# Two-block transformer kernel: the running sum of the later modulation rows goes from VectorE to ScalarE and GpSimd

## The chip, the core and the metric

The kernel runs on one core of one Trainium2 chip. The metric is device time in microseconds (us) of one launch, median of a few runs. The engines are named as in the profile: PE is TensorE (PEld its weight loads), ACT is ScalarE, DVE is VectorE, POOL is GpSimd and SP is SyncE, which issues most of the DMAs. Each engine works through its own instructions in order and meets the others only through semaphores.

## What is computed

The reference runs two blocks on 256 tokens of width 2048. What matters here is the first, and in it the modulation: one row vector times a 2048 x 12288 matrix.

```python
mod = c_act @ w_ada[layer] + b_ada[layer]            # c_act = silu(c), one row of 2048
sh1, sc1, gt1, sh2, sc2, gt2 = jnp.split(mod[:, None, :], N_MOD, axis=-1)
h = rmsnorm(x, g_mix[layer]) * (1 + sc1) + sh1
x = x + (1 + gt1) * mixer(h, positions, ...)          # sb attention, dsa attention, merge, w_o
h = rmsnorm(x, g_ffn[layer]) * (1 + sc2) + sh2
x = x + (1 + gt2) * conv_ffn(h, ...)
```

`sh1` and `sc1` are needed before anything else. The other four parts, 8192 columns, are needed only after the merge, so the kernel computes them beside the attentions: this is the "late" work.

## The kernel before

Weights are f32. For each unit (128 x 2048 of a weight matrix, 1 MB, loaded by SP into one of up to four slots of `ring`) ACT rounds it in two halves of 128x1024 to `whi` (`round_unit`, L355), DVE subtracts to get the rest `wlo` (`rest_unit`, L362), and PE multiplies in three passes (`threefold`, L415 to L417). `whi` and `wlo` hold two units. A half of unit u may be rounded once PE is through the same half of unit u-2, and semaphore `used` says so. `ahead` rounds the first two units of the next iteration.

The first block's mixer has three stages in which late work runs.

- `sb`: five passes of a loop body over four pairs of heads. Pass i projects pair i (units 0 to 5) and attends pair i-1.
- `dsa`: the same for the second attention, after a stage for its index (`ki`, `qi`).
- `merge`: eight iterations of six units. In each, ACT takes two pairs of sigmoids (L1480) behind its rounding; the first pair and the second pair of banks are then combined by DVE.

The late work is 16 blocks of 512 columns. Block b has 16 lines of 128x512 (one for each 128 rows of `w_ada`), and one block falls into each iteration: blocks 0 to 3 in `sb`, 4 to 7 in `dsa`, 8 to 15 in `merge`. POOL issues the load of each line (`late_loads`, L2435) into `late_ring`, which has four slots. DVE multiplies the line by its column of `cact` and adds it to the only accumulator, `late_acc` (`late`, L1816 for line 0, L1819 for the others). A slot is loaded again when DVE has used it (`late_used`). When all 16 lines are in, PE adds up the partitions (`late_sum`, L763), at a fixed place in its order: behind units 0 and 1 of the next iteration. Until then line 0 of the next block may not overwrite `late_acc`, and semaphore `late_summed` guards that.

DVE's calls of `late` lie between its `rest_unit` calls: in `sb` lines 0 to 2, 3 to 5, 6 to 10 and 11 to 15; in `dsa` 0 to 5, 6 to 10, 11 to 15; in `merge` four lines behind each of units 2 to 5. All loops over lines are unrolled; the loops over iterations are partly peeled.

## Time and profile before

| | |
|---|---|
| median of 3 runs | 3329.79 us (3328.99 to 3337.11) |
| the profiled execution | 3330.51 us, its span 3328.8 us |
| mean granted TensorE clock | 0.943 of full speed |
| busy: PE / DVE / ACT / POOL | 2976.4 / 2033.2 / 1361.2 / 173.0 us |
| `sb` stage | about 128 to 300 us |
| `dsa` stage | about 420 to 595 us |
| `merge` stage | about 605 to 905 us |

The profile page of the kernel before gives busy time by engine, a timeline in 40 slices, the DMA queues, the chain of work that ended last and the costliest groups of instructions. Time is read from the span's start. Late work exists only before 905 us; what follows (`wo`, `up`, `down` and the second block) is not touched.

### The profile page before, as it was taken

How to read it: one execution, taken by the hardware profiler on the slowest of the kernel's cores; microseconds unless marked ns; L12 is line 12 of the kernel's file. 1: busy time of each engine (PE TensorE's matmuls, PEld its weight loads, DVE VectorE, ACT ScalarE, POOL GpSimd, SP SyncE). 2: the span in 40 equal slices, each digit the busy share in tenths (PEclk: the TensorE clock that was granted, in tenths of full speed). 3: DMA queues.
4: the chain of work that ended last, by engine and by line, in shares of the span. 5: the costliest groups of instructions: out<-in, count | busy, mean ns of one | idle time of the engine just before them, and what ended most of it. 6: DMA issues, size and time to landing. Idle time of an engine off the chain costs nothing.

```text
span 3328.8 us, 61772 instructions
## 1 busy us (share of the span) xinstructions
PE 2976.4 (89%) x24632; PEld 2815.9 (85%) x24632; DVE 2033.2 (61%) x2768; ACT 1361.2 (41%) x1917; POOL 173.0 (5%) x287
## 2 busy tenths in 40 slices
PE   2698699799998999999998999849698999999997
PEld 1698688799997888888996999848696999999996
DVE  7774777677656666665445544476556555555445
ACT  1354233333345555554434334412244444444443
POOL 0121012122100000000000000012000000000000
PEclk6798899899999999999998999979898999999999
DMA  9775277688754555554552555400152555554552
GB/s 364 279 255 157 89 231 235 213 298 279 259 183 134 189 186 185 184 190 164 188 179 89 177 164 177 123 2 4 52 177 89 181 185 185 181 189 165 182 184 88
DMA packets 407390, 585.26 MB, mean 176 GB/s; under 512 B 20384, under 2 KB 368672, under 8 KB 389856
## 3 DMA queue, kind: packets, MB, share of 16 engines
q1 hardware_dynamic: 384720, 516.22, 46.8%
q0 software_dynamic: 20480, 67.13, 5.9%
q8 instruction: 92, 1.51, 0.2%
q10 hardware_dynamic: 2064, 0.13, 0.0%
q14 instruction: 34, 0.28, 0.0%
HBM read 581.33 MB, written 2.10 MB: 175 GB/s over the span
## 4 chain that ended last, share of the span: by engine, by line
PE 75%; DVE 13%; DMA 6%; issue 3%; ACT 2%; DVEq 0%; POOLq 0%; ACTq 0%; POOL 0%; SPq 0%
PE bank L415 16%; PE bank L416 16%; PE bank L417 16%; PE bank L422 15%; PE bank L423 8%; DMA late_ring<-w_ada_dram 4%; PE bank L1048 3%; DVE wlo L362 3%; DVE work L1819 2%; PE bank L674 1%; DVE work L1788 1%; DMA ring<-w_ada_dram 1%; ACT whi L355 1%; DVE mats L2204 0%; DVE hraw L715 0%
## 5 line engine op out<-in xcount | busy, mean ns | idle before, releaser
L362 DVE TENSOR_TENSOR wlo<-ring,whi 128x1024 fp32r<-128x1024 f32 x908 | 1085.7, 1220 | 636.3 <-ACT whi L355 635.3
L355 ACT ACTIVATE whi<-ring 128x1024 fp32r<-128x1024 f32 x908 | 943.9, 1054 | 1132.9 <-PE bank L417 742.1
L415 PE MATMUL bank<-hx,whi 128*128 128x256 f32 (+2 forms) x2704 | 781.2, 289 | 66.0 <-DVEq L533 30.2
L416 PE MATMUL bank<-hx,whi 128*128 128x256 f32 (+2 forms) x2704 | 777.2, 287 | 0.0
L417 PE MATMUL bank<-hx,wlo 128*128 128x256 f32 (+2 forms) x2704 | 777.0, 287 | 0.0
L422 PE MATMUL bank<-hx,whi 128*128 128x512 f32 x2112 | 741.9, 395 | 7.4 <-DVE hx L721 7.4
L423 PE MATMUL bank<-hx,wlo 128*128 128x256 f32 x2112 | 592.3, 280 | 0.0
L415 PEld LDWEIGHTS bank<-hx,whi 128*128 128x128 f32 x2704 | 520.9, 193 | 70.8 <-DVEq L533 31.0
L415 PE MATMUL bank<-xs,whi 128*128 128x256 f32 (+1 forms) x1920 | 545.1, 284 | 35.8 <-DVE xs L408 35.2
L416 PE MATMUL bank<-xs,whi 128*128 128x256 f32 (+1 forms) x1920 | 545.3, 284 | 0.0
L417 PE MATMUL bank<-xs,wlo 128*128 128x256 f32 (+1 forms) x1920 | 545.1, 284 | 0.0
L416 PEld LDWEIGHTS bank<-hx,whi 128*128 128x128 f32 x2704 | 520.9, 193 | 0.0
L417 PEld LDWEIGHTS bank<-hx,wlo 128*128 128x128 f32 x2704 | 518.7, 192 | 0.0
L422 PEld LDWEIGHTS bank<-hx,whi 128*128 128x128 f32 x2112 | 397.4, 188 | 100.8 <-DVE hx L721 7.8
L423 PEld LDWEIGHTS bank<-hx,wlo 128*128 128x128 f32 x2112 | 398.3, 189 | 0.0
L415 PEld LDWEIGHTS bank<-xs,whi 128*128 128x128 f32 x1920 | 363.6, 189 | 37.1 <-issue 37.1
L416 PEld LDWEIGHTS bank<-xs,whi 128*128 128x128 f32 x1920 | 368.2, 192 | 0.0
L417 PEld LDWEIGHTS bank<-xs,wlo 128*128 128x128 f32 x1920 | 364.4, 190 | 0.0
L408 DVE TENSOR_TENSOR xs<-work,xs 128x256 fp32r<-128x256 f32 (+1 forms) x136 | 56.6, 428 | 302.7 <-ACT xs L398 302.7
L1819 DVE SCALAR_TENSOR_TENSOR work<-late_ring,cact,work 128x512 f32<-128x512 f32 x240 | 180.3, 751 | 86.7 <-DMA late_ring<-w_ada_dram 73.8
L398 ACT ACTIVATE xs<-work 128x256 fp32r (+2 forms) x136 | 55.0, 418 | 428.2 <-PE bank L417 398.4
L2435 POOL DMA_DIRECT2D late_ring<-w_ada_dram x256 | 137.5, 537 | 755.0 <-DVE work L1816 345.6
(269 smaller groups left out, 2676.8 us busy)
## 6 DMA issues: line engine op xcount, KB each, us to landing
ring<-w_in_dram SPq DMA_DIRECT2D x136, 1024.0 KB, 5.4
ring<-w_up_dram SPq DMA_DIRECT2D x88, 1024.0 KB, 5.0
ring<-w_down_dram SPq DMA_DIRECT2D x88, 1024.0 KB, 4.8
ring<-w_gate_up_dram SPq DMA_DIRECT2D x88, 1024.0 KB, 5.0
late_ring<-w_ada_dram POOLq DMA_DIRECT2D x256, 256.0 KB, 4.1
ring<-w_ada_dram SPq DMA_DIRECT2D x32, 1024.0 KB, 7.5
ring<-w_o_dram SPq DMA_DIRECT2D x16, 1024.0 KB, 5.0
ring<-w_out_dram SPq DMA_DIRECT2D x16, 1024.0 KB, 5.2
```

The lines of the kernel that those rows point to most:

```text
L355: nc.scalar.activation(half_of(whi, u, h, n), ring[:, u % PLAN[phase][3], h * n // 2:(h + 1) * n // 2], ACT.Copy)\
L362: nc.vector.tensor_tensor(half_of(wlo, u, h, n), ring[:, u % PLAN[phase][3], h * n // 2:(h + 1) * n // 2], half_of(whi, u, h, n).bitcast(F ...
L398: last = nc.scalar.activation(xhi[:, u % 2, at:at + n], src, ACT.Copy)
L408: last = nc.vector.tensor_tensor(xlo[:, u % 2, at:at + n], src, xhi[:, u % 2, at:at + n].bitcast(F32), ALU.subtract)
L415: nc.tensor.matmul(out_ap, a[0], b[0], start=start, stop=False, **kw)
L416: nc.tensor.matmul(out_ap, a[0], b[1], start=False, stop=False, **kw)
L417: return nc.tensor.matmul(out_ap, a[1], b[0], start=False, stop=stop, **kw)
L422: nc.tensor.matmul(bank[:, b, :].rearrange("p (a t) -> p a t", a=2), a[0], x, start=start, stop=False, **kw)
L423: return nc.tensor.matmul(bank[:, b, 0:T], a[1], x[:, 0, :], start=False, stop=stop, **kw)
L1048: return nc.tensor.matmul(out_ap, a, b, start=start, stop=stop, skip_group_check=True)
L1819: ins = nc.vector.scalar_tensor_tensor(late_acc, src, cact[:, j:j + 1], late_acc, ALU.mult, ALU.add)
L2435: nc.gpsimd.dma_start(late_ring[:, j % NSLOT:j % NSLOT + 1, :], v).then_inc(late_landed[j % NSLOT], 16)
```

## The change

ACT scales each line in its own ring slot, with the column of `cact` as the scale. POOL adds line 1 to line 0 and each further line to `late_acc`, waits for its own add, and then issues the load that goes into the freed slot. The four slots, the one accumulator and PE's `late_sum` stay as they are. DVE no longer touches late lines.

```diff
+            def late(b, j0, j1):                                   # ScalarE
+                for j in range(j0, j1):
+                    n = j % NSLOT
+                    act.wait_ge(late_landed[n], b * (16 * KD // NSLOT) + 16 * (j // NSLOT + 1))
+                    nc.scalar.activation(late_ring[:, n, :], late_ring[:, n, :], ACT.Copy, scale=cact[:, j:j + 1]).then_inc(late_scaled, 1)
...
                     round_unit("sb", 2, i)
+                    late(i, 0, 2)
                     round_unit("sb", 3, i)
+                    late(i, 2, 4)
...
                     round_unit("sb", 4, i)
+                    late(i, 4, 7)
                     round_unit("sb", 5, i)
+                    late(i, 7, 10)
...
                 if head:
+                    late(i, 10, 13)
                     ahead(round_unit, "sb", i, last)
+                    late(i, 13, KD)
...
                 for u in range(2, 6):
                     round_unit("merge", u, i)
+                    late(i + 8, 4 * (u - 2), 4 * (u - 1))
...
-            def late(b, j0, j1):                                   # VectorE, with all its calls
...
-                    if j == 0:
-                        if not first(b):
-                            dve.wait_ge(late_summed, b)
-                        ins = nc.vector.tensor_scalar(late_acc, src, cact[:, j:j + 1], None, ALU.mult)
-                    else:
-                        dve.wait_ge(late_used, b * KD + j)
-                        ins = nc.vector.scalar_tensor_tensor(late_acc, src, cact[:, j:j + 1], late_acc, ALU.mult, ALU.add)
-                    ins.then_inc(late_used, 1)
...
+            def late(b, last):                                     # GpSimd
+                for j in range(KD):
+                    n = j % NSLOT
+                    pool.wait_ge(late_scaled, b * KD + (j + 1))
+                    if j == 0:
+                        continue
+                    if j == 1:
+                        if not first(b):
+                            pool.wait_ge(late_summed, b)
+                        nc.gpsimd.tensor_tensor(late_acc, late_ring[:, 0, :], late_ring[:, 1, :], ALU.add).then_inc(late_used, 2)
+                    else:
+                        nc.gpsimd.tensor_tensor(late_acc, late_acc, late_ring[:, n, :], ALU.add).then_inc(late_used, 1)
+                    pool.wait_ge(late_used, b * KD + (j + 1))
+                    for m in ((0, 1) if j == 1 else (j,)):
+                        if m < KD - NSLOT:
+                            late_load(b, m + NSLOT)
+                        elif not last:
+                            late_load(b + 1, m + NSLOT - KD)
+            for j in range(NSLOT):
+                late_load(0, j)
+            rotated(pool, NLATE, late)
```

In `dsa` the calls on ACT stand at the same places as in `sb`, with block i + 4.

## Rows read from the trace of the kernel before

**Rows 1.** The page's groups: busy, mean ns of one, idle before and its releaser.

```profile
L362 DVE TENSOR_TENSOR wlo<-ring,whi 128x1024 fp32r<-128x1024 f32 x908 | 1085.7, 1220 | 636.3 <-ACT whi L355 635.3
L1819 DVE SCALAR_TENSOR_TENSOR work<-late_ring,cact,work 128x512 f32<-128x512 f32 x240 | 180.3, 751 | 86.7 <-DMA late_ring<-w_ada_dram 73.8
```

**Rows 2.** Busy by stage: us, PE, PEld, DVE, ACT, POOL (instructions), clock, DMA share, GB/s.

```profile
128.00:300.00 172.00, 154.80 (x1227) 150.93 (x1226) 118.16 (x151) 89.89 (x106) 36.62 (x68) 0.96 0.79 251
420.00:595.00 175.00, 150.88 (x1169) 148.02 (x1169) 136.67 (x193) 60.42 (x91) 34.34 (x64) 0.91 0.74 236
605.00:905.00 300.00, 287.16 (x2368) 284.91 (x2368) 220.52 (x275) 111.87 (x129) 66.53 (x124) 0.98 0.83 276
```

**Rows 3.** Stretches from one late sum to the next: merge's mean of six, sb, dsa.

```profile
sum 222.10, PE 214.79 PEld 213.00 DVE 164.78 ACT 82.93 POOL 51.51; mean PE 35.80 PEld 35.50 DVE 27.46 ACT 13.82 POOL 8.58
...
209.90:250.80 40.90, 39.64 (x327) 39.13 (x326) 30.05 (x38) 22.05 (x26) 8.59 (x16) 1.00 0.79 258
462.40:506.40 44.00, 40.29 (x319) 39.70 (x318) 34.88 (x50) 16.00 (x24) 8.58 (x16) 0.96 0.74 239
```

**Rows 4.** PE's order in merge: start, us, engine, line; idle before and releaser.

```profile
605.51 0.55 PE L415 MATMUL bank<-ys,whi 128*128 128x256 f32 x1 [9.04 <-DVE ys L1975]
...
713.26 0.38 PE L415 MATMUL bank<-ys,whi 128*128 128x256 f32 x1 [0.29 <-DVE wlo L362]
724.71 0.95 PE L763 MATMUL bank<-ones,work 128*128 128x1 f32 x8
...
874.90 0.95 PE L763 MATMUL bank<-ones,work 128*128 128x1 f32 x8
900.68 1.05 PE L763 MATMUL bank<-ones,work 128*128 128x1 f32 x8 [1.69 <-ACT work L1480]
```

**Rows 5.** POOL's only two-input operation: by line (ns min/median/max), then by form.

```profile
L2451 POOL TENSOR_TENSOR spare<-mats,consts x23: 1263/1268/1804, 2204.0 to 2330.6; 128x512 f32<-128x512 f32 x23
...
L2451 POOL TENSOR_TENSOR spare<-mats,consts 128x512 f32<-128x512 f32 x23 | 32.6, 1422 | 113.9 <-PE bank L1048 65.2 <-DVE mats L2204 48.7
```

**Rows 6.** POOL and DVE side by side near 2239: start, us.

```profile
2239.46 1.39 POOL L2451 TENSOR_TENSOR spare<-mats,consts 128x512 f32<-128x512 f32 x1 [3.42 <-PE bank L1048]
...
2239.64 1.76 DVE L2192 TENSOR_TENSOR work<-spare,work 128x512 f32<-128x512 f32 x1
```

**Rows 7.** DVE's line 0 in merge and POOL's two loads behind it: start, us.

```profile
725.77 0.49 DVE L1816 TENSOR_SCALAR work<-late_ring,cact 128x512 f32<-128x512 f32 x1 [4.22 <-PE bank L763]
...
726.90 0.54 POOL L2435 DMA_DIRECT2D late_ring<-w_ada_dram  x1 [14.40 <-DVE work L1816]
727.69 0.54 POOL L2435 DMA_DIRECT2D late_ring<-w_ada_dram  x1 [0.25 <-issue]
```

**Rows 8.** Late loads from issue to landing, in sb, in dsa, in merge.

```profile
DMA to landing us min/median/max: 2.9/3.9/6.8
...
DMA to landing us min/median/max: 2.9/3.5/5.8
...
DMA to landing us min/median/max: 2.9/4.5/7.3
```

**Rows 9.** ACT by form: busy, mean ns of one (512 wide; 272 wide with a scale column).

```profile
L1614 ACT ACTIVATE work<-work 128x512 f32<-128x512 f32 x4 | 2.5, 617 | 0.0
L1572 ACT ACTIVATE work<-bank,omu 128x272 f32<-128x272 f32 x24 | 10.2, 475 | 0.0
```

**Rows 10.** ACT's order: in sb near 219.6, in merge near 737.

```profile
219.57 3.88 ACT L355 ACTIVATE whi<-ring 128x1024 fp32r<-128x1024 f32 x4
...
737.16 1.06 ACT L355 ACTIVATE whi<-ring 128x1024 fp32r<-128x1024 f32 x1 [1.78 <-PE bank L417]
738.12 0.64 ACT L1480 ACTIVATE work<-bank 128x256 f32<-128x256 f32 x2
```

**Rows 11.** A long PE wait in merge, and the five us behind it.

```profile
825.20 0.57 PE L415 MATMUL bank<-ys,whi 128*128 128x256 f32 x1 [3.79 <-DVE wlo L362]
...
825.00:830.00 5.00, 4.80 (x22) 4.81 (x23) 4.80 (x8) 0.00 (x0) 0.00 (x0) 0.50 0.68 199
```

More of the change, by code:

```diff
@@ L292, in build @@
         late_landed = [sem(f"late_landed{n}") for n in range(NSLOT)]
-        late_used, late_summed = sem("late_used"), sem("late_summed")
+        late_scaled, late_used, late_summed = sem("late_scaled"), sem("late_used"), sem("late_summed")
         lora_landed, gate_landed = sem("lora_landed"), sem("gate_landed")
@@ L1445, in dsa @@
                     round_unit("dsa", 2, i)
+                    late(i + 4, 0, 2)
                     round_unit("dsa", 3, i)
+                    late(i + 4, 2, 4)
                 if tail:
@@ L1455, in dsa @@
                     round_unit("dsa", 4, i)
+                    late(i + 4, 4, 7)
                     round_unit("dsa", 5, i)
+                    late(i + 4, 7, 10)
                 if tail:
@@ L1461, in dsa @@
                 if head:
+                    late(i + 4, 10, 13)
                     ahead(round_unit, "dsa", i, last)
+                    late(i + 4, 13, KD)
                 if tail:
@@ L1805, in _ @@
             phase_end(dve, 2)
-            def late(b, j0, j1):
-                for j in range(j0, j1):
-                    n = j % NSLOT
-                    dve.wait_ge(late_landed[n], b * (16 * KD // NSLOT) + 16 * (j // NSLOT + 1))
-                    src = late_ring[:, n, :]
-                    if j == 0:
-                        if not first(b):
-                            dve.wait_ge(late_summed, b)
-                        ins = nc.vector.tensor_scalar(late_acc, src, cact[:, j:j + 1], None, ALU.mult)
-                    else:
-                        dve.wait_ge(late_used, b * KD + j)
-                        ins = nc.vector.scalar_tensor_tensor(late_acc, src, cact[:, j:j + 1], late_acc, ALU.mult, ALU.add)
-                    ins.then_inc(late_used, 1)
             def overlapped(body, count, per):
@@ L1845, in sb @@
                     nc.vector.tensor_copy(qT[:].rearrange("p a t -> p (a t)"), bank[:, 0, :]).then_inc(q_read, 1)
-                    late(i, 0, 3)
                     rest_unit("sb", 4, i)
@@ L1854, in sb @@
                 if head:
-                    late(i, 3, 6)
                     rest_unit("sb", 5, i)
@@ L1865, in sb @@
                 if head:
-                    late(i, 6, KD if last else 11)
                     ahead(rest_unit, "sb", i, last)
@@ L1871, in sb @@
                     nc.vector.tensor_copy(vS[:].rearrange("p a t -> p (a t)"), bank[:, 2, :]).then_inc(v_read, 1)
-                    if not last:
-                        late(i, 11, KD)
             overlapped(sb, 4, 0)
@@ L1957, in dsa @@
                 if head:
-                    late(i + 4, 0, 6)
                     rest_unit("dsa", 5, i)
@@ L1961, in dsa @@
                     rope(kT[:].rearrange("p a t -> p (a t)"), bank[:, 1, :], 2 * T, tabs128, 64, k2_read, i + 1)
-                    late(i + 4, 6, KD if last else 11)
                     ahead(rest_unit, "dsa", i, last)
@@ L1967, in dsa @@
                     nc.vector.tensor_copy(vS[:].rearrange("p a t -> p (a t)"), bank[:, 2, :]).then_inc(v2_read, 1)
-                    if not last:
-                        late(i + 4, 11, KD)
             overlapped(dsa, 4, 10)
@@ L1980, in merge @@
                     rest_unit("merge", u, i)
-                    late(i + 8, 4 * (u - 2), 4 * (u - 1))
                 for s in range(2):
```

11 lines of the change are left out of this document (4 added, 7 removed).

## The prediction

> **What bounds the kernel now.** The first thing to look at is busy time by stage, since late work exists only before 905 us. In `sb` PE is busy 154.8 of 172 us, in `dsa` 150.9 of 175, in `merge` 287.2 of 300 [rows 2]. PE sets the pace in all three; without its idle time they would be 17.2, 24.1 and 12.8 us shorter. DVE is busy 69%, 78% and 74% there, ACT 52%, 35% and 37%. So the averages say that ACT has room and DVE less, which is what speaks for the change.
>
> The second thing is the loop that late work closes, because averages don't show it. `late_acc` exists once. PE sums it at a fixed place behind units 0 and 1 of an iteration, and the next block may not touch it before. DVE waited there for PE, in the iteration at 725 us for 4.22 us [rows 7], and did the 16 lines within the iteration all the same. From one late sum to the next the iteration takes 40.9 us in `sb`, 44.0 in `dsa`, and 222.1 / 6 = 37.0 in `merge` [rows 3]. Whether the change is faster or slower is decided by whether the new route of a line closes this loop within those times.
>
> **Part by part.** *Removed from DVE*: 240 operations of 0.751 us [rows 1] and 16 of 0.49 [rows 7], 188 us, and 86.7 us of waiting in front of them. Almost none of it is on PE's path, which has only the idle time above to give back.
>
> *Added to ACT*: 256 scalings of 128x512. 512 wide without a column is 0.617 us, 272 wide from a bank with a column 0.475 [rows 9]. Both ways of reading that give 0.62 to 0.85; I take 0.75, near the row of the same width. That is 192 us. ACT's busy time in `merge` rises from 112 to about 208 of 300, so its load isn't the trouble. Its order is: ACT waits for the landing of every line, and behind it are queued the rounding of the next unit, the sigmoids, and in the attentions the exponentials.
>
> *Added to POOL*: 240 adds. The trace has POOL's only two-input operation at the same size, 1.263 to 1.804 us [rows 5]; the mean is 1.422. Beside DVE it isn't alone: the DVE operation that starts 0.18 us into a POOL operation takes 1.76 us, and ends 0.55 us behind POOL's end [rows 6], so the two take turns. DVE's two-input subtractions are 12 per iteration at 1.22 us [rows 1], 14.6 of some 50 us, so a POOL add waits for one 29% of the time, on average half of one: 0.18 us. 1.27 + 0.18 agrees with 1.42, which I take. Bounds: 1.27 alone, and 1.27 + 1.22 behind a whole subtraction.
>
> By the Trainium skill (GPSIMD Engine Reference, section 3.1, elementwise cycle accounting) a POOL `tensor_tensor` costs about 2.6 cycles per element at 1.2 GHz, so 512 elements would be 1.11 us as an estimate, and the page's advice is to leave such adds to VectorE. The row of the same size shows 1.27 at best; by the page's figure a line would be 0.31 us cheaper than I take, and a merge period 3.4 us shorter. The same page (section 8, key points) says that POOL shares its SBUF interfaces with VectorE when that has two SBUF inputs; the trace agrees, with the 1.76 us above.
>
> *POOL's period per line*, p. POOL does not issue the load before its own add has ended. From the end of DVE's line 0 (726.26) to the load that waits for it is 0.64 us, and the load holds POOL 0.54; loads behind each other are 0.25 apart [rows 7]. So p = 1.42 + 0.64 + 0.54 + 0.05 (my estimate for picking up the next add) = 2.65 us. Bounds: 1.27 + 0.40 + 0.54 = 2.21, if some of the 0.64 is address work done ahead, and 3.2, if adds mostly stand behind a subtraction or behind the making of the load's descriptors. Before, DVE did a line in 0.75 and POOL's loads ran beside it.
>
> *The loop in merge*. ACT can't round unit 0 of the next iteration before it has scaled line 15. Line 15 goes into the slot that line 11 left, so 11 adds must be done, and the first of them waits for the late sum. From one late sum to the next:
>
> late sum 0.95 [rows 4] + POOL wakes 0.40 (estimate: 0.64 less a part) + 11 p = 29.15 + a second load behind the first add 0.79 [rows 7] + landing 4.5 - 0.54 = 3.96 [rows 8] + scaling 0.75 + two sigmoids 0.64 and half a rounding 1.06 [rows 10] + the subtraction and hand-overs 1.22 + 0.20 [rows 1] + units 0 and 1 on PE, 713.26 to 724.71 = 11.45 [rows 4] = 50.6 us.
>
> To this comes the clock. PE waited 3.79 us at 825.2, and in the 5 us behind it the granted clock was 0.50 of full, the 1.2 GHz level, with 22 matmuls [rows 11]. At the upper level one takes 39.64 / 327 = 0.121 us [rows 3], so 41 would fit, and the wait costs 19 x 0.121 = 2.3 us more; I take 2.5. In the new loop PE stands for about 5 us ahead of units 4, 5 and 0; the last wait is on the loop, so 53.1 us per iteration against 37.0. Six periods: +96.6. The first iteration: PE begins at 605.5 [rows 4], ACT scales lines 0 and 1 by 613.9 (behind unit 2's rounding, which follows PE's first unit), and with the same terms unit 0 is ready at 613.9 + 29.15 + 8.62 = 651.7, where PE would be there at 605.5 + six units of 11.45 / 2 = 639.9: +11.8, with the clock +14.3. The last: 25.8 us from late sum to late sum (874.90 to 900.68, [rows 4]) become 0.95 + 0.40 + 29.15 + 0.79 + 3.96 + 0.75 + one add 1.82 = 37.8: +12.0. `merge` together: +122.9.
>
> *sb*. Here lines 10 to 12 are scaled ahead of the next iteration's unit 0, so line 12 is the last on the loop, and it needs 8 adds. Lines 4 to 6 come behind unit 4's rounding, which ends 11.6 us behind the late sum (ACT's four halves begin at 219.57, [rows 10], the sum at 209.9). Adds 1 to 3 are done by then; from line 4's scaling: 12.4 + 5 p = 25.6, landing less 0.54 = 29.0 [rows 8], scaling 29.8, rounding and subtraction 32.2, units 0 and 1 and the scores' products (1.3) 45.0. Against 40.9: +4.1, clock +2.5, and +1.4 for line 3, which then comes too late to fit ahead of the exponentials. Two periods: +16. In the first iteration loads and adds have no loop constants (p about 2.35), unit 0 comes 7.5 us late and with the clock 10. In the last pass the exponentials stand behind line 15, but DVE, which now is 5 us late with its own late lines there, is not: +5. Together +31.
>
> *dsa*. The same loop, but unit 4's rounding comes early, so: 0.95 + 0.40 + 8 p = 21.2 + 0.79 + 2.96 + 0.75 + 1.06 + 1.42 + 11.45 + 1.3 + 2.5 = 44.8 against 44.0. Today's 44.0 holds a PE wait of 3 to 4.5 us behind DVE, which the change removes; the ring's wait takes its place. Two periods +1.6, first +3, last +4: +9.
>
> *Free*: POOL's wait for `late_scaled` and the moved loads have nothing behind them, as POOL has no other work before 905 us. SP's queue is not passed.
>
> The sum: 122.9 + 31 + 9 = +162.9 us, against the profiled execution's 3330.51: 3493.4. That execution lies 0.7 us from the median of the runs, which I neglect.
>
> **Rivals.**
>
> *The ring is quicker* (p = 2.21, no clock loss). Merge period 21.4 + 24.3 = 45.7, so 6 x 8.7 = 52, first 7, last 7; `sb` +14; `dsa` -7, since its PE needs some 41 us for an iteration. +73: 3403 us. For it: part of the 0.64 may be hidden, and only one wait in `merge` shows the low clock. Chance 0.21, with all between 3385 and 3450.
>
> *The shared interface and the load's descriptors weigh more* (p = 3.2, the subtraction 0.6 longer). Period 59.8, 6 x 22.8 = 137, first 19, last 18, `sb` +43, `dsa` +28: +245, 3575 us. For it: [rows 6] shows both sides losing. Against: at most 29% of POOL's adds should meet a subtraction. Chance 0.20, for 3535 to 3610.
>
> *DVE's relief decides* (faster). The place is PE's idle time: 17.2 + 24.1 + 12.8, less the 9 us at the start of `merge`, which stay, leaves 45, of which the scores and the last passes' chains keep some; I put it at -40: 3290 us. It decides as soon as the loop is shorter than PE's own work: 21.4 + 11 p < 37.0, so p < 1.41 us. An add and a load that follow each other are 1.27 + 0.54 = 1.81 by the fastest rows. It would take adds that overlap loads inside POOL, against the wait in the code. Chance 0.06.
>
> *The change does nothing that can be measured*, because ring waits and relief cancel: 3330 us, chance 0.03. Between that and the quick ring 0.04; above all 0.01.
>
> **How the numbers follow.** The forecast (p from 2.4 to 2.9, 3450 to 3535) has a chance of 0.45, and the predicted time is its middle, 3493.4. The range takes in the quick and the heavy ring, 3390 to 3590, and leaves out some 0.15. A measurement of this kernel can tell about 0.3% (10 us) from no change. Faster 0.06, same 0.03, slower 0.91.
>
> **What would show it.** Right: in `merge` PE waits for `wlo` ahead of units 4, 5 and 0, some 5 us each, and late sums lie about 53 us apart; ACT's scaling waits for DMA `late_ring`; POOL's adds last 1.3 to 2.5 us, with a load 0.64 behind each; DVE's subtractions get longer than 1.22 beside them; `sb` and `dsa` grow much less than `merge`; the time behind `merge` stays as it is. Wrong: PE waits for `late_sum` instead of `wlo` (then POOL's 15 adds are the bound, not the ring), loads that start less than 0.3 us behind an add, scalings far over 0.75 us, or late sums 37 us apart.

## The result, and the profile after

| | before | after |
|---|---|---|
| median | 3329.94 us (4 runs, 3328.99 to 3337.11) | 3436.79 us (4 runs, 3432.33 to 3442.6) |
| ratio | | 1.0317, 95% interval 1.0296 to 1.0338 |
| span of the profiled execution | 3328.8 us | 3435.0 us |
| mean granted TensorE clock | 0.943 | 0.933 |

The change makes the kernel 107 us slower. The forecast was 3493, so sign and stated range (3390 to 3590) hold, but the loss is two thirds of the one forecast, and 3436.8 lies outside the forecast's own band (3450 to 3535), in the one that the prediction gave to the quicker ring (3385 to 3450). Where it lies is read from PE's rows, by the same marks in both traces: the start of `dsa` (the row with a 19.9 us wait in front, 405.65 before and 420.79 after), the start of `merge` (605.51 and 618.95), and the late sums.

| step | predicted | measured |
|---|---|---|
| `sb`, first late sum | +10 | +7.7 |
| `sb`, two periods | +16 | +4.3 |
| `sb`, last pass up to `dsa` | +5 | +3.2 |
| `dsa`, first late sum | +3 | -0.2 |
| `dsa`, two periods | +1.6 | -2.2 |
| `dsa`, last pass up to `merge` | +4 | +0.6 |
| `merge`, first late sum | +14.3 | +10.9 |
| `merge`, six periods | +96.6 | +78.3 |
| `merge`, last period | +12.0 | +8.0 |
| all behind | 0 | -4.4 |

So 97.2 of the 106.2 us between the two profiled executions are lost in `merge`. The 4.4 us gained behind it were not followed up. The view of several stretches, from one late sum to the next, shows how; its columns are those of [rows 2], and the four lines answer to [rows 3]: the six periods of `merge` together, the one of them that is followed below, one of `sb`, one of `dsa`.

```profile
sum 300.50, PE 240.01 PEld 236.37 DVE 133.06 ACT 141.64 POOL 170.50; mean PE 40.00 PEld 39.39 DVE 22.18 ACT 23.61 POOL 28.42
...
776.10:824.90 48.80, 39.52 (x300) 38.91 (x298) 22.29 (x19) 23.70 (x32) 28.52 (x31) 0.90 0.68 214
...
218.90:262.80 43.90, 41.38 (x328) 40.74 (x326) 28.55 (x22) 32.13 (x42) 29.61 (x31) 0.96 0.74 239
477.40:521.20 43.80, 40.48 (x320) 39.64 (x319) 36.38 (x34) 25.89 (x41) 28.43 (x31) 0.96 0.74 236
```

A period of `merge` is now 300.50 / 6 = 50.08 us where it was 37.02. PE is idle 10 us of it, and no engine is full: DVE is busy 44%, ACT 47%, POOL 57%. That is what a loop over several engines looks like, and the averages alone say that there is room everywhere. In `sb` a period is 43.9 (40.9 before), in `dsa` 43.8 (44.0).

The chain of work that ended last, of one period, is the loop itself. Each line is start, us, and what. Of the ten similar rounds one is shown.

```profile
by line: POOL work L2441 26.6%; issue 15.2%; POOL late_ring L2428 11.0%; PE bank L415 8.3%; PE bank L416 7.8%; PE bank L417 7.8%; DMA late_ring<-w_ada_dram 6.1%; DVE wlo L362 5.4%; POOL work L2439 5.2%; PE bank L763 3.2%; ACT whi L355 1.9%;
...
776.28 0.80 PE bank L763 x8
777.25 1.31 POOL work L2439
...
795.65 1.31 POOL work L2441
797.07 0.49 issue
797.60 0.55 POOL late_ring L2428
...
803.15 1.48 POOL work L2441
804.74 0.49 issue
805.25 3.05 DMA late_ring<-w_ada_dram
```

Behind the late sum POOL adds, stands still for about 0.6 us until its own add has been signalled, issues the load, and takes the next add. Adds start 2.53 us apart ((803.15 - 780.36) / 9). The 11th releases the load of line 15. PE's rows of the same period, as in [rows 4]:

```profile
776.11 0.95 PE L763 MATMUL bank<-ones,work 128*128 128x1 f32 x8
...
790.84 0.39 PE L415 MATMUL bank<-hx,whi 128*128 128x256 f32 x1 [2.32 <-DVE wlo L362]
...
803.52 0.58 PE L415 MATMUL bank<-hx,whi 128*128 128x256 f32 x1 [5.22 <-DVE wlo L362]
...
813.40 0.38 PE L415 MATMUL bank<-ys,whi 128*128 128x256 f32 x1 [1.74 <-DVE wlo L362]
...
824.87 0.95 PE L763 MATMUL bank<-ones,work 128*128 128x1 f32 x8
```

PE waits in three places, ahead of units 4, 5 and 0, and each time for `wlo`, never for POOL. Who stands behind `wlo` is in the waits of `merge` (engine and line, waited for, us in all, times, longest):

```profile
DVE wlo L362 <- ACT whi L355: 184.9, 46, 10.0
ACT late_ring L1392 <- DMA late_ring<-w_ada_dram: 150.4, 67, 5.7
POOL work L2439 <- PE bank L763: 76.7, 7, 11.6
PE bank L415 <- DVE wlo L362: 71.2, 23, 6.4
```

PE waits for DVE, DVE for ACT's rounding, ACT for a late line's landing, and that landing hangs on POOL's add of four lines earlier. POOL waits 76.7 us at the late sums, some 11 us each, so its adds alone don't fill the period. What closes the loop is the order on ACT: line 15 has to be scaled before unit 0 is rounded.

The page's groups have the sizes. They answer to [rows 1], [rows 5] and [rows 9].

```profile
PE 3006.4 (88%) x24632; PEld 2846.2 (83%) x24632; DVE 1981.7 (58%) x2512; ACT 1518.1 (44%) x2173; POOL 495.7 (14%) x527
...
L362 DVE TENSOR_TENSOR wlo<-ring,whi 128x1024 fp32r<-128x1024 f32 x908 | 1202.6, 1348 | 874.4 <-ACT whi L355 873.1
...
L2441 POOL TENSOR_TENSOR work<-work,late_ring 128x512 f32<-128x512 f32 x224 | 297.0, 1326 | 15.1 <-ACT late_ring L1392 10.3
L1392 ACT ACTIVATE late_ring<-late_ring,cact 128x512 f32<-128x512 f32 x256 | 177.1, 717 | 240.9 <-DMA late_ring<-w_ada_dram 240.4
```

DVE lost 188 us of work, yet its busy time fell by 51.5 us only (2033.2 to 1981.7). The rest went into its own operations, 117 us of it into the subtraction of the page (1085.7 before [rows 1], 1202.6 now). The duration of the subtraction (min/median/max ns) in `dsa`, of the kernel before:

```profile
L362 DVE TENSOR_TENSOR wlo<-ring,whi x48: 1216/1219/1227, 412.4 to 587.7; 128x1024 fp32r<-128x1024 f32 x48
```

and of the kernel after:

```profile
L362 DVE TENSOR_TENSOR wlo<-ring,whi x48: 1209/2373/2749, 427.6 to 599.2; 128x1024 fp32r<-128x1024 f32 x48
```

The same instruction, at the median, takes twice as long once POOL adds beside it. Busy time of the whole `dsa` stage, before:

```profile
405.65:605.50 199.85, 166.69 (x1272) 163.52 (x1273) 144.77 (x197) 67.98 (x97) 34.34 (x64) 0.89 0.66 210
```

and after:

```profile
420.80:618.90 198.10, 166.24 (x1272) 162.12 (x1272) 149.38 (x133) 106.94 (x161) 114.65 (x124) 0.91 0.66 212
```

DVE runs 64 operations fewer there, 47 us by [rows 1] and [rows 7], and is busy 4.6 us more.

### The profile page after: what moved, and what is told of

The parts are those of the page before. It is cut to its first block, busy times and chain, and to the rows that moved or that the text cites. A ratio compares the mean times of both kernels' runs of the same rounds, so it can differ in the third digit from the quotient of the medians.

```text
span 3435.0 us, 61741 instructions
## 1 busy us (share of the span) xinstructions
PE 3006.4 (88%) x24632; PEld 2846.2 (83%) x24632; DVE 1981.7 (58%) x2512; ACT 1518.1 (44%) x2173; POOL 495.7 (14%) x527
## 4 chain that ended last, share of the span: by engine, by line
PE 71%; DVE 9%; POOL 8%; issue 5%; DMA 4%; ACT 3%; POOLq 0%; ACTq 0%; DVEq 0%; SPq 0%
PE bank L415 15%; PE bank L416 15%; PE bank L417 14%; PE bank L422 14%; PE bank L423 7%; POOL work L2441 5%; PE bank L1048 3%; POOL late_ring L2428 2%; DMA late_ring<-w_ada_dram 2%; DVE wlo L362 2%; PE bank L674 1%; DMA ring<-w_ada_dram 1%; ACT whi L355 1%; DVE work L1808 1%; DVE mats L2199 0%
## 5 line engine op out<-in xcount | busy, mean ns | idle before, releaser
L362 DVE TENSOR_TENSOR wlo<-ring,whi 128x1024 fp32r<-128x1024 f32 x908 | 1202.6, 1348 | 874.4 <-ACT whi L355 873.1
L415 PE MATMUL bank<-hx,whi 128*128 128x256 f32 (+2 forms) x2704 | 794.1, 294 | 123.6 <-DVE wlo L362 71.8
L416 PE MATMUL bank<-hx,whi 128*128 128x256 f32 (+2 forms) x2704 | 787.8, 291 | 0.0
L417 PE MATMUL bank<-hx,wlo 128*128 128x256 f32 (+2 forms) x2704 | 786.9, 291 | 0.0
L415 PEld LDWEIGHTS bank<-hx,whi 128*128 128x128 f32 x2704 | 532.4, 197 | 131.0 <-DVE wlo L362 76.1
L416 PEld LDWEIGHTS bank<-hx,whi 128*128 128x128 f32 x2704 | 532.6, 197 | 0.0
L417 PEld LDWEIGHTS bank<-hx,wlo 128*128 128x128 f32 x2704 | 529.7, 196 | 0.0
L422 PEld LDWEIGHTS bank<-hx,whi 128*128 128x128 f32 x2112 | 397.3, 188 | 98.3 <-DVE hx L721 7.8
L423 PEld LDWEIGHTS bank<-hx,wlo 128*128 128x128 f32 x2112 | 399.6, 189 | 0.0
L2441 POOL TENSOR_TENSOR work<-work,late_ring 128x512 f32<-128x512 f32 x224 | 297.0, 1326 | 15.1 <-ACT late_ring L1392 10.3
L1392 ACT ACTIVATE late_ring<-late_ring,cact 128x512 f32<-128x512 f32 x256 | 177.1, 717 | 240.9 <-DMA late_ring<-w_ada_dram 240.4
```

The costliest lines, as they stand in the source:

```text
L362: nc.vector.tensor_tensor(half_of(wlo, u, h, n), ring[:, u % PLAN[phase][3], h * n // 2:(h + 1) * n // 2], half_of(whi, u, h, n).bitcast(F ...
L415: nc.tensor.matmul(out_ap, a[0], b[0], start=start, stop=False, **kw)
L416: nc.tensor.matmul(out_ap, a[0], b[1], start=False, stop=False, **kw)
L417: return nc.tensor.matmul(out_ap, a[1], b[0], start=False, stop=stop, **kw)
L422: nc.tensor.matmul(bank[:, b, :].rearrange("p (a t) -> p a t", a=2), a[0], x, start=start, stop=False, **kw)
L423: return nc.tensor.matmul(bank[:, b, 0:T], a[1], x[:, 0, :], start=False, stop=stop, **kw)
```

## The experiments

The theory: a small ring, one accumulator and ACT's order close a loop that is longer than PE's work. Rival A: ACT's waits for lines do it, whoever adds. Rival B: POOL's adds do it, through the interface that they share with DVE. Every ratio is against the kernel before on the same chip. Stage times are given as `dsa` start / `dsa` length / `merge` up to the last late sum; before they are 405.65 / 199.9 / 295.2, after 420.79 / 198.2 / 392.4. They are of the profiled execution, the other times of the median.

**One half of the change alone: ACT scales, DVE adds.** DVE gets its calls of `late` back at the old places, as a plain add; POOL only loads.

```diff
+                        nc.vector.tensor_tensor(late_acc, late_ring[:, 0, :], late_ring[:, 1, :], ALU.add).then_inc(late_used, 2)
...
+                    ins = nc.vector.tensor_tensor(late_acc, late_acc, late_ring[:, n, :], ALU.add)
```

> ScalarE scales the lines in their slots as in the changed kernel; the adds are VectorE's again, at the places where it had its multiply-and-add, and GpSimd only issues loads, each as soon as its slot is free. Theory (GpSimd's serial add, wait, load of 2.5 us per line closes the loop from late sum to late sum, 50 us in merge): an add is 0.69 us on VectorE and the loads run beside it, so most of the loss goes: 3345 us, 3325 to 3375. Rival A (ScalarE, which waits for each line's landing ahead of the rounding, is what costs): the loss stays, 3410 to 3440. Rival B (the shared SBUF interface): no GpSimd adds, so 3330 to 3345.

Measured: 1.0168 (1.0149 to 1.0186), 3380.5 us, 5 us above my range; stages 424.0 / 222.6 / 311.4. In `merge` the loss falls from 97 to 16 us: taking POOL's serial add and load out of the loop opens it, as the theory has it, though with the adds the contact at the shared interface goes too, so this run alone doesn't tell the theory from rival B. But the attentions become 41 us slower than before, which I had not expected. The durations of the adds, and PE's row in `dsa`:

```profile
L1840 DVE TENSOR_TENSOR work<-work,late_ring x224: 680/692/696, 138.7 to 953.2; 128x512 f32<-128x512 f32 x112
...
570.72 0.58 PE L415 MATMUL bank<-hx,whi 128*128 128x256 f32 x1 [6.15 <-DVE wlo L362]
```

An add of 0.692 us is hardly cheaper than the multiply-and-add of 0.751 [rows 1], so DVE is relieved of next to nothing, and now two engines with a fixed order wait for each other's lines: ACT stood 85.3 us for landings in `dsa`, DVE 41.9 us for ACT's scalings. Rival A has its share in the attentions of this kernel and is false in `merge`.

**The other half alone: DVE scales in the slot, POOL adds.**

```diff
-                    nc.scalar.activation(late_ring[:, n, :], late_ring[:, n, :], ACT.Copy, scale=cact[:, j:j + 1]).then_inc(late_scaled, 1)
+                    nc.vector.tensor_scalar(late_ring[:, n, :], late_ring[:, n, :], cact[:, j:j + 1], None, ALU.mult).then_inc(late_scaled, 1)
```

> The other half of the change: GpSimd adds and loads as in the changed kernel, VectorE scales the lines in their slots at its old places, ScalarE does nothing with them. Theory (GpSimd's 2.5 us per line): the loop is as long as with ScalarE's scaling, merge about 50 us per iteration, 3430 us, 3405 to 3460. Rival A (ScalarE's waits): 3330 to 3370. Rival B (the shared interface): VectorE's scaling meets GpSimd's adds too, 3440 or more.

Measured: 1.0565 (1.0548 to 1.0583), 3512.9 us, 188 us above before and worse than the whole change; stages 448.2 / 248.6 / 401.1 (of an execution of 3527 us, 14 above the median). PE now stands for POOL at eight of its late sums, 4 to 21 us each, as here:

```profile
321.96 1.87 PE L763 MATMUL bank<-ones,work 128*128 128x1 f32 x8 [14.66 <-POOL work L2438]
```

My 3430 is missed by 83 us, and the time lies where I had put rival B (3440 or more). DVE, which still has a late operation for every line, pays for POOL's adds and waits for the ring. So it is not ACT's scaling that makes the change slow. Taking it away from ACT makes matters worse, and POOL's adds in the ring are the costly part.

**Half the add.** From line 2 on, POOL adds columns 0 to 255 only; the rest of the sum is left out.

```diff
-                        nc.gpsimd.tensor_tensor(late_acc, late_acc, late_ring[:, n, :], ALU.add).then_inc(late_used, 1)
+                        nc.gpsimd.tensor_tensor(late_acc[:, 0:LATE // 2], late_acc[:, 0:LATE // 2], late_ring[:, n, 0:LATE // 2], ALU.add).then_inc(late_used, 1)
```

> The changed kernel with GpSimd's adds from line 2 on over half of the columns, 256 of 512; the other half of the sum is left out. Theory: an add falls from 1.33 to 0.7 us, the period per line from 2.5 to 1.9, and 11 lines lie on the loop in merge, so an iteration falls from 50 to 43 us; 7.5 such iterations give 52 us, the attentions 5 to 10 more: 3376 us, 3360 to 3395. If the loop were closed by landings or by ScalarE's own work, the adds would be beside it: 3420 to 3437. If VectorE's wait at the shared interface were the cost: half the overlap, about 3420.

The adds of `merge` (busy, mean ns, idle before):

```profile
L2441 POOL TENSOR_TENSOR work<-work,late_ring 128x256 f32<-128x256 f32 x112 | 86.5, 772 | 8.7 <-ACT late_ring L1392 6.3
```

Measured: 1.0099 (1.0082 to 1.0116), 3356.5 us, 3.5 us below my range; stages 403.2 / 179.6 / 346.9. Each of these adds is 0.53 us shorter on the mean (0.772 against 1.306 of the changed kernel in `merge`). Eleven adds stand on the loop, and ten of them are of this kind, as the first keeps its width: 5.3 us. The period of `merge` falls by 7.06 (50.08 to 43.02). That is the theory's slope, and the rows show where most of the other 1.7 us are. The subtraction ahead of unit 0, which is on the loop too, took 2.1 to 2.7 us in the six periods of the changed kernel, 2.5 on the mean; with half adds it takes 1.23 again in four of the six. Units 0 and 1 fall from 12.4 to 11.7 us, as the low clock meets them less often. So the shared interface costs some 1.3 us of each period of `merge` (2.5 less 1.22), by lengthening one subtraction on the loop.

In `dsa` the stage takes 179.6 us, 18.6 less than with the change and 20 less than before. Subtractions are back at a median of 1226 ns, and DVE is busy 112.29 instead of 149.38 us. But the loop is shorter here as well, and this run changes both at once. The chain of one period of the changed kernel in `dsa` has the ring on it, eight adds from the late sum to the load of line 12, and behind the landing one long subtraction:

```profile
478.49 1.31 POOL work L2439
...
498.77 4.14 DMA late_ring<-w_ada_dram
...
504.63 2.21 DVE wlo L362
```

Seven of the eight adds are halved, 0.48 us each by the means in this stage (1.322 less 0.839), 3.4 us together, and the two periods fell by 4.6 on the mean. So the ring is the larger part there too. The subtraction (2.21 instead of 1.22) and a wait of PE for DVE of 1.2 us ahead of L917, which neither the kernel before nor this one has in these periods, bound the interface's part at some 2 us per period.

**Loops written out.** PE's and POOL's loops over iterations are written out, so that POOL's addresses are constants.

```diff
-            rotated(pool, NLATE, late)
+            for b in range(NLATE):
+                late(b, b == NLATE - 1)
```

> The changed kernel with GpSimd's and TensorE's loops over blocks and iterations written out, so that no address or wait value is computed in registers between an add and the load behind it. Theory: the 0.64 us from an add's end to its load falls to about 0.3, as in the peeled first block, the period per line from 2.5 to 2.2; merge loses 11 x 0.33 = 3.6 us per iteration, 27 in all, and the attentions 3 to 8: 3406 us, 3395 to 3420. If what GpSimd does between the adds isn't on the path: 3430 to 3440. TensorE's written-out code could cost some us by fetching instructions.

Measured: 1.0231 (1.0212 to 1.0249), 3403.6 us; stages 421.12 / 191.5 / 370.9. From an add's end to the load is 0.30 us (64.7 us in 218 waits) where it was 0.61 (133.7 in 218). Eleven times the difference is 3.4 us, and the period fell by 4.1, to 45.99, with adds as long as before. The prediction had 0.64 for this gap and called 0.40 its lower bound "if some of it is address work": with constants it is lower still.

**A second accumulator on top.** Blocks take turns between two accumulators, so that POOL may begin a block ahead of the late sum of the one before.

```diff
-                            pool.wait_ge(late_summed, b)
+                            pool.wait_ge(late_summed, b - 1)
```

> The kernel with written-out loops (e4_both_unrolled, 1.0231 of before) with a second accumulator, used by every other block, so that GpSimd's first add of a block no longer waits for TensorE's late sum of the block before. Theory (the loop is closed by the one accumulator and the place of the late sum): GpSimd can begin a block when ScalarE has scaled its first lines, some 5 us ahead of the late sum, and only its own 15 x 2.2 = 33 us and the four slots are left; merge falls from 46.0 to about 41.5 us per iteration, 30 to 35 us in all: ratio 1.013, 1.008 to 1.017. If the ring's four slots and ScalarE's order alone close the loop: 1.020 to 1.024.

Measured: 1.0173 (1.0152 to 1.0194), 3390.2 us; stages 418.63 / 186.5 / 358.8; `merge` period 45.0. Taking the late sum out of the loop gains 1 us per period where I had expected 4.5. The waits of the stretch from 600 to 935 us say why:

```profile
POOL work L2440 <- ACT late_ring L1393: 94.2, 8, 24.9
```

POOL no longer waits for the late sum, but it waits for ACT instead, once in each of the eight blocks, because ACT scales no line while it rounds the two units of `ahead`. In this order of ACT the single accumulator was not what held the loop.

**The order on ACT.** The same, and in `merge` ACT takes three lines behind each of units 2 to 5, two behind the two units of `ahead` and two behind the last pair of sigmoids, where it took four behind each of units 2 to 5 and none later.

```diff
-                    late(i + 8, 4 * (u - 2), 4 * (u - 1))
+                    late(i + 8, 3 * (u - 2), 3 * (u - 1))
...
                         ahead(round_unit, "merge", i, last)
+                        late(i + 8, 12, 14)
...
+                late(i + 8, 14, KD)
```

> The kernel with two accumulators and written-out loops (e5_two_accumulators, 1.0173 of before; merge 45.0 us per iteration), and in merge ScalarE scales its 16 lines spread over all six units, 3, 3, 3, 3, 2 and 2, in place of 4 behind each of units 2 to 5. Theory (what is left of the loop in merge is the four slots: a batch of four takes GpSimd 4 x 2.2 us and a landing, while ScalarE stands in front of the next rounding; two units of 5.7 us go without any line): merge falls to 39 to 41.5 us, 28 to 48 us in all: ratio 1.006, 1.003 to 1.010. If VectorE's subtractions, longer beside GpSimd's adds, close the loop: no change, 1.014 to 1.019.

Measured: 1.0020 (1.0010 to 1.0030), 3339.7 us; stages 413.5 / 190.6 / 311.0, better than I had expected. A period, and the last late sum:

```profile
650.90:688.60 37.70, 35.54 (x300) 35.17 (x298) 25.37 (x18) 22.73 (x32) 31.29 (x32) 1.00 0.84 270
...
915.10 1.83 PE L763 MATMUL bank<-ones,work 128*128 128x1 f32 x8 [10.30 <-POOL work L2444]
```

This period takes 37.7 us at the full granted clock, the six together 38.2 on the mean, against 37.0 before. Of the 16 us that `merge` still loses, 9 are at the end, where PE waits 10.3 us for POOL's last adds, and 7 in the six periods.

**The order alone.** The changed kernel, with that edit of ACT's order and nothing else.

> The changed kernel (1.0317 of before, merge 50.1 us from late sum to late sum), one accumulator, loops as they are; only ScalarE's lines in merge are spread over the six units, 3, 3, 3, 3, 2 and 2, in place of 4 behind each of units 2 to 5. Theory (the batches ahead of the next iteration's rounding close the loop): line 11, not line 15, stands ahead of unit 0, so GpSimd's 15 adds at 2.5 us between two late sums are the next bound, 39 to 42 us per iteration: 60 to 80 us less, ratio 1.010, 1.006 to 1.016. If the gain of e12_lines_spread (1.0020) needed the second accumulator and the shorter period per line: 1.020 to 1.028.

Measured: 1.0156 (1.0139 to 1.0172), 3381.5 us; stages 425.3 / 198.3 / 332.8; `merge` period 41.6. The order of ACT's calls alone gives back about half of the loss (107 us fall to 52), 8.5 us per period. It also changes who is late:

```profile
880.80 1.05 PE L763 MATMUL bank<-ones,work 128*128 128x1 f32 x8 [1.07 <-POOL work L2443]
...
956.44 1.84 PE L763 MATMUL bank<-ones,work 128*128 128x1 f32 x8 [9.90 <-POOL work L2443]
```

Now PE waits at its late sums for POOL, whose serial work now binds: 3.11 to the second add, 13 x 2.53 = 32.9 to the last, 1.3 for that, late sum and wake-up 1.3, together 38.6 of the 41.6 us. In the period before 880.80 a further 2.7 are one load that starts 3.32 us behind its add instead of 0.64; what held it the trace doesn't name (more on such loads below). In this order the second accumulator and the shorter gap do pay: with both, the period is 38.2. The levers depend on each other: each measured alone has the value that the other bounds leave to it.

**What idle adds cost.** The kernel before, and behind every fourth late load POOL makes three adds of 128x512 on a tile that nobody uses. Nobody waits for them but POOL.

```diff
+                            nc.gpsimd.tensor_tensor(scratch, consts[:, 0:LATE], consts[:, LATE:2 * LATE], ALU.add).then_inc(idle_added, 1)
```

> The kernel before, and behind every fourth late load GpSimd adds three times on a tile that nobody uses (128x512, 192 adds of about 1.3 us; a load may start 1 to 3 us later). No wait is added for another engine. It prices the shared SBUF interface alone. My theory: VectorE's two-input operations that meet an add are longer, up to 1.3 us each, but TensorE is ahead by several us in sb and merge, so it costs little, 5 to 20 us: ratio 1.004, 1.001 to 1.007. Rival (the interface, not the serial chain, makes the loss): with 192 adds for the change's 240 the ratio would be 1.020 or more.

Measured: 1.0374 (1.0357 to 1.0391), 3455.9 us. I had expected 1.004; the rival had 1.020 or more. DVE's groups of 128 to 1000 us, and the adds of the whole run:

```profile
L363 DVE TENSOR_TENSOR wlo<-ring,whi 128x1024 fp32r<-128x1024 f32 x200 | 323.7, 1663 | 70.0 <-ACT whi L356 69.5
L1821 DVE SCALAR_TENSOR_TENSOR work<-late_ring,cact,work 128x512 f32<-128x512 f32 x228 | 255.2, 1119 | 47.6 <-DMA late_ring<-w_ada_dram 35.4 <-DVE work L1821 1.9
L2442 POOL TENSOR_TENSOR work<-consts 128x512 f32<-128x512 f32 x192 | 320.4, 1669 | 11.1
```

**The same time in clearings.** Nine clearings of the unused tile in place of the three adds, POOL's loop written out (with the idle adds it was not). Its late loads take the columns of block 0 in every block, the same amount of data.

```diff
+                            nc.gpsimd.memset(scratch, 0.0).then_inc(idle_added, 1)
```

> The control to e10_idle_adds (1.0374 of before): the kernel before, and in place of three idle adds GpSimd clears the same unused tile nine times (0.5 us each, so about as long as the three adds), with its loop over the blocks written out so that the waits are constants. Loads are held up as before. Theory: the 124 us of e10 come from two-input operations of VectorE and GpSimd that take turns at the shared interface, and a clearing reads nothing: ratio 1.001, 0.998 to 1.006. If loads that start later were the cost: 1.02 to 1.037. If writes collide too: between them.

```profile
L363 DVE TENSOR_TENSOR wlo<-ring,whi 128x1024 fp32r<-128x1024 f32 x228 | 269.0, 1221 | 87.8 <-ACT whi L356 87.3
L1821 DVE SCALAR_TENSOR_TENSOR work<-late_ring,cact,work 128x512 f32<-128x512 f32 x240 | 180.3, 751 | 117.0 <-DMA late_ring<-w_ada_dram 106.1 <-DVE work L1821 1.4
L2442 POOL MEMSET work<- 128x512 f32 x576 | 304.6, 529 | 29.5
```

Measured: 1.0077 (1.0062 to 1.0092), 3359.3 us, above the 1.006 that I had allowed. POOL is about as busy (304.6 against 320.4 us), and neither of DVE's two groups is longer: 1221 and 751 ns, the sizes of before. DVE waits 106.1 us for late lines instead of 73.8, so the 26 us most likely come from loads that POOL issues later. The other 98 us of the kernel with idle adds come with adds in the place of clearings, and DVE's operations of 1663 and 1119 ns show how: 192 adds, with no one waiting for their result, cost nearly as much as the whole change. This holds for a kernel in which DVE also keeps its 256 late operations; in the changed kernel it has none of them to be lengthened.

**The new route in `dsa` alone.** `dsa` is the stage where PE waited for DVE before (4.47, 3.26, 2.98 us). Blocks 4 to 7 go by ACT and POOL, with POOL's part written out; `sb` and `merge` stay as they were.

```diff
+            for b in range(4, 8):
+                late(b)
+            with pool.Fori(8, NLATE) as b:
+                late_loads(b)
```

> The new route in the dsa stage alone (blocks 4 to 7, GpSimd's loop over them written out); in sb and merge lines go VectorE's old way. Theory: dsa is the stage in which TensorE waited for VectorE before (24 us idle of 175), and GpSimd's period of 2.2 us per line just fits its 41 us, so the stage gains 6 to 10 us as in e4_both_unrolled (191.5 against 199.9 us) and nothing else moves: ratio 0.9975, 0.996 to 0.9995. If the change costs everywhere by its load on the shared interface: above 1.000.

Measured: 0.9977 (0.9968 to 0.9986), 3324.8 us; `dsa` 192.0 us, 7.8 less than before.

**And with half of the columns left on DVE.** ACT and POOL take 256 columns, DVE multiplies and adds the other 256, at places nearer to ACT's. POOL loads a slot again when its own add and DVE's half are both done.

```diff
+                        ins = nc.vector.scalar_tensor_tensor(to, src, cact[:, j:j + 1], to, ALU.mult, ALU.add)
```

> As e7_dsa_only, but in dsa each line is split: ScalarE and GpSimd take its left 256 columns, VectorE multiplies and adds the right 256 as before, in places nearer to ScalarE's. GpSimd's period falls to about 1.6 us per line, and its adds meet VectorE half as long. With half adds the dsa stage took 179.6 us instead of 199.9, with VectorE free of late lines; here VectorE keeps 64 operations of 0.42 us. Theory: 182 to 190 us for the stage, ratio 0.996, 0.994 to 0.998. If VectorE's in-order waits for landings are what cost in dsa (not its busy time): 1.000 or more.

Measured: 1.009 (1.0076 to 1.0104), 3362.7 us; `dsa` 233.5 us. A miss: shorter operations, and 41 us more. The waits of `dsa` have

```profile
ACT late_ring L1394 <- DMA late_ring<-w_ada_dram: 112.2, 31, 10.1
POOL late_ring L2462 <- DVE work L1848: 77.9, 16, 10.8
DVE work L1848 <- DMA late_ring<-w_ada_dram: 14.5, 13, 3.8
```

POOL stands 77.9 us for DVE's halves before it may load, and ACT 112.2 us for the landings. Each slot now needs two engines, both with a fixed order, before it is loaded again. It is the lock-step of the first experiment once more, as far as these waits show.

**`dsa` alone, with a second accumulator** for blocks 4 and 6. PE's loop over the iterations of `dsa` is written out here too, so the step from the run with one accumulator holds both.

> The new route in dsa alone (e7_dsa_only, 0.9977 of before, dsa 192.1 us) with a second accumulator for blocks 4 and 6. With two accumulators everywhere dsa took 186.5 us. Theory: another 4 to 6 us: ratio 0.9962, 0.9950 to 0.9975. If the second accumulator only moves the wait to the ring: 0.9977 again.

Measured: 0.9961 (0.9947 to 0.9975), 3318.9 us; `dsa` 186.2 us. It is the best version here, 13 us faster than the kernel before on the same chip and 3.4% faster than the change. The subtraction in `dsa`:

```profile
L362 DVE TENSOR_TENSOR wlo<-ring,whi x48: 1210/1464/2341, 413.4 to 574.7; 128x1024 fp32r<-128x1024 f32 x48
```

## Why the prediction was right, and where its sum was off

*The loop and its place.* Right for `merge` and `dsa`. The forecast was that PE waits for `wlo` ahead of units 4, 5 and 0, that ACT's scaling waits for landings, and that nearly all is lost in `merge`. The rows show each, with waits of 2.3, 5.2 and 1.7 us where I had written some 5 for all three. The chain of one period runs through the terms of the sum, in its order. Half adds moved the period by 7.06 where ten shorter adds make 5.3 and the subtraction some 1 more, and the written-out loop by 4.1 where eleven shorter gaps make 3.4.

The forecast was 57 us too high: 26 in `merge`, 16 in `sb`, 11 in `dsa`, 4 behind them. All of its errors but that of the subtraction point the same way, so they add up, and the range holds the result only because it takes in the quicker ring as well.

*The terms of the period of `merge`*, from the period at 776.11:

| term | predicted | measured |
|---|---|---|
| late sum | 0.95 | 0.95 |
| POOL wakes | 0.40 | 0.19 |
| first add to line 15's load | 29.35 | 28.00 |
| landing, from the load's start | 4.5 | 3.08 |
| line 15's scaling to PE's unit 0 | 3.87 | 5.07 |
| units 0 and 1 | 11.45 | 11.47 |
| clock | 2.5 | 0 |
| sum | 53.1 | 48.8 |

The period per line was 2.53 and not 2.65: an add took 1.31 here and not the 1.42 of [rows 5]. I had put 0.18 on it for standing behind subtractions, and it is the subtraction that mostly gives way. The 5.07 us hold the first of these two, some 2.6 instead of 1.22:

```profile
810.58 5.21 DVE L362 TENSOR_TENSOR wlo<-ring,whi 128x1024 fp32r<-128x1024 f32 x2 [0.47 <-ACT whi L355]
```

The landing was taken from [rows 8], the median of a stretch where 276 GB/s moved. The slower kernel moves 209 in `merge`, and the median there fell from 4.5 to 3.1. As far as these two show, a loss thins the traffic, and that gives some of it back.

*The clock* was put at 2.5 us on each of `merge`'s six periods, and on several of the other steps; it cost 1.0 on the mean. Beside these 1.5 us too many stand 1.35 for the adds and 1.4 for the landing, less 1.2 for the subtraction. The wait is there, and so is the low clock behind it (columns of [rows 2]):

```profile
803.50:808.50 5.00, 4.98 (x23) 4.98 (x24) 2.19 (x1) 1.78 (x4) 3.65 (x5) 0.50 0.54 167
813.40:818.40 5.00, 5.00 (x42) 5.00 (x43) 5.00 (x5) 1.59 (x3) 1.84 (x2) 1.00 0.50 154
```

Behind the wait of 5.22 us at 803.5 the granted clock is 0.50, the 1.2 GHz level, with 23 matmuls in 5 us; behind the wait of 1.74 us at 813.4 it is 1.00, with 42. I had put some 5 us ahead of unit 0, and it was 1.7. The low clock fell on unit 5, after which PE waits for unit 0 anyway, so there it cost nothing: an engine that is slow ahead of its own wait is slow for free. In four of the six periods units 0 and 1 took 12.8 to 13.0 instead of 11.5 us, at a mean granted clock of 0.87 to 0.88, and that is all it cost. This makes 48.8 + 1.0 on the mean. The other 0.4 are one period of 52.5 us, with a load that starts 3.32 us behind its add instead of 0.64:

```profile
906.51 0.55 POOL L2428 DMA_DIRECT2D late_ring<-w_ada_dram  x1 [3.32 <-issue]
```

Together they are 50.2, and 50.1 were measured. The kernel before has such a load as well, at 817.46, 2.92 us late, and DVE's wait of 3.15 us for its landing lies ahead of the PE wait of 3.79 us of [rows 11]. So the row from which I took the price of the clock was itself the trace of a late load.

*`sb`*, +31 predicted and +15 measured. A period was to be 8 us longer (4.1 by the ring, 2.5 by the clock, 1.4 by line 3), and the two are 1.4 and 2.9 longer. The ring's wait ahead of unit 0 is there in the first (1.42 us, no low clock behind it) and missing in the second. There PE stands 2.52 us for DVE's part of the scores instead of 1.26, and is busy 41.38 instead of 39.64 us at a granted clock of 0.96. So the mechanism of the sum holds in half of `sb`'s periods; which of its terms was too long there I did not follow. In the first iteration PE waits 6.1 us for `wlo`.

*`dsa`*, +9 predicted and -1.7 measured. "The ring's wait takes the place" of the wait for DVE was right: the periods are 43.8 and 42.2 against 44.0 and 44.2, predicted 44.8, with PE waits of 5.1, 2.0 and 1.9 us ahead of unit 0, and the chain has the ring's eight adds on it. What the sum left out is that DVE's 47 us of relief went into longer operations. Of these the loop holds one subtraction (2.2 and 1.8 us instead of 1.22), and PE waits 1.2 us per period for another DVE operation.

*The last late sums* (37.8 predicted in `merge`) came after 33.75 us with a wait of 4.02 us, and not for POOL but for ACT:

```profile
1011.32 1.87 PE L763 MATMUL bank<-ones,work 128*128 128x1 f32 x8 [4.02 <-ACT work L1500]
```

In `sb` the one at 304.85 waited 11.2 us for POOL, where it had waited 2.1 us for DVE; the score chain that follows was late anyway, and the stage ends only 3.2 us later by it.

*The rivals.* The quick ring (3403) had a shorter p and no clock: its second half was nearly true, its first only with the loop written out, and that kernel measured 3403.6. The heavy interface (p = 3.2) was false for p, but the subtraction was longer by more than its 0.6 us. Rival B of the experiments is the larger part where DVE also keeps its lines (3455.9 us with idle adds); in the changed kernel it has some 1.3 us of each `merge` period and at most some 2 in `dsa`. By the Trainium skill (GPSIMD Engine Reference, section 3.1) an add of this size would be an estimated 1.11 us; POOL's adds here have a median of 1.30, so the row, not the page, is the value to take. The relief of DVE did decide in `dsa` once the loop there was short, 7.8 us for the stage with the new route there alone, 13.6 with a second accumulator and PE's loop written out. It did so in no other stage. That nothing measurable changes was false by a factor of ten.

*What stays open*: the interface's share of the 107 us as a whole. In `merge` the long subtraction on the loop makes some 8 us of the 78 of its periods; in the attentions it is bounded, not measured. Every way to shorten the adds shortens the ring's loop too, and adds of the same length without two inputs, at the same place, were not tried. Nor is it known what holds a load for 3 us.

## What to carry to other kernels

Before moving work to an engine with room, write down the loop that its buffers, its accumulator and the fixed order of each engine close, and compare it with the period of the engine that sets the pace: here 11 x 2.5 us of a serial add and load decided, and no busy share showed it. An engine that prepares work for the bound engine must not stand in a row of foreign lines ahead of it; spreading the same 16 lines over six places instead of four gave back half of the loss. And use the new route only in the stage where the bound engine really waits for the relieved one: in `dsa` alone, with a second accumulator, it gained 13 us.

## What the runs showed of the hardware

- A POOL add with two inputs in SBUF and a DVE operation with two inputs in SBUF lengthen each other: DVE's 128x1024 subtraction went from 1.22 to a median of 2.37 and at most 2.75 us, POOL's 128x512 add from 1.27 alone to 1.67 on the mean. Two inputs are not needed on DVE's side. With DVE's scaling and POOL's adds, DVE's multiplication of one SBUF tile by a column, 0.48 us alone, took up to 2.12:

```profile
L1812 DVE TENSOR_SCALAR late_ring<-late_ring,cact x256: 471/486/2119, 135.2 to 1095.8; 128x512 f32<-128x512 f32 x128
```

- POOL's clearings lengthened neither the subtractions nor the multiply-and-adds. The same one-input multiplication took up to 0.77 us in that run, where it took at most 0.49 before.
- POOL's adds did not lengthen DVE operations with one input in a bank. Two neighbours in `dsa`, of the changed kernel, 0.69 us each before, show it (busy, mean ns, idle before). Two of L1886's eight ran beside an add for their whole length, and took 0.69 us; four of L1887's did, and took 2.07 to 2.33:

```profile
L1887 DVE TENSOR_TENSOR work<-work 128x512 f32<-128x512 f32 x8 | 11.8, 1476 | 0.3
...
L1886 DVE TENSOR_TENSOR work<-bank,work 128x512 f32<-128x512 f32 x8 | 5.5, 692 | 0.3
```

- The price does not depend on anybody waiting for the adds: 192 unused ones cost some 98 us more than clearings of about the same time.
- Now and then a load that POOL issues starts late with nothing shown that it waits for. In `merge` there is one in each of six kernels looked at: 2.92 us before, 3.32 with the change and with its order alone changed, 2.97 in the three with written-out loops.
- From the end of a POOL add to the load that waits for it are 0.61 us when the addresses come from a loop, and 0.30 us when they are constants.
- An in-place scaling of 128x512 on ACT takes 0.717 us, a plain DVE add of the same size 0.692 us and DVE's fused multiply-and-add 0.751 us: splitting the two costs nearly twice the engine time.
